# A decoder layer on one core: the last down-projection group made four tiles deep, and the next stage's first weights and rows prepared under its visits

## The reference, cut to what matters

```
gate, up = split(rmsnorm(h, g_ffn) @ w_gate_up)          # 2 x 5632 wide
h = h + (silu(gate) * up) @ w_down                       # "down"
h = h + sigmoid(rmsnorm(h, g_ple) @ w_ple_gate) * (p_i @ w_ple_proj)
y = rmsnorm(h, g_final)                                  # p_i is 256 wide
```

## Time and profile before

| | |
|---|---|
| median of 3 runs | 2339.3 us (2337.1 to 2341.42) |
| the profiled execution, its own time | 2344.21 us |
| span of the profiled execution | 2342.4 us |
| PE busy | 2270.8 us, 97% |
| DVE busy | 1639.2 us, 70% |
| ACT busy | 1080.8 us, 46% |
| POOL busy | 191.8 us, 8% |
| mean granted TensorE clock | 0.99 |

### The profile page before, as it was taken

How to read it: one execution, slowest core, us unless ns; L and a number is a source line. 1 busy time by engine, 2 the same in 40 slices (tenths; PEclk the granted TensorE clock), 3 DMA queues, 4 the chain that set the end, 5 groups by cost and what they waited for, 6 DMA issues and landing times.

```text
span 2342.4 us, 45807 instructions
## 1 busy us (share of the span) xinstructions
PE 2270.8 (97%) x18549; PEld 2219.8 (95%) x18549; DVE 1639.2 (70%) x2125; ACT 1080.8 (46%) x1639; POOL 191.8 (8%) x88
## 2 busy tenths in 40 slices
PE   7999999999999999999999999999899999989997
PEld 6988898888999999999999999999899999979997
DVE  5355555564257888888888888888777777885333
ACT  5334444443245455454445454554434444564434
POOL 0041112301221000000000000000000000121111
PEclk9999999999999999999999999999999999999999
DMA  7454565543334445454554545457966865532332
GB/s 251 141 167 155 163 195 179 175 122 128 93 90 150 119 134 171 139 171 139 161 149 136 160 132 161 136 171 224 299 178 191 235 179 148 148 90 82 88 107 80
DMA packets 488018, 359.44 MB, mean 153 GB/s; under 512 B 8417, under 2 KB 469298, under 8 KB 487001
## 3 DMA queue, kind: packets, MB, share of 16 engines
q1 hardware_dynamic: 474921, 347.31, 50.2%
q10 hardware_dynamic: 13000, 10.78, 1.4%
HBM read 301.23 MB, written 57.29 MB: 153 GB/s over the span
## 4 chain that ended last, share of the span: by engine, by line
PE 91%; DVE 4%; DMA 2%; ACT 2%; issue 1%; SPq 0%; ACTq 0%; DVEq 0%
PE acc L1161 39%; PE acc L718 30%; PE scores L1161 15%; PE scores L718 2%; PE mail_bank L718 1%; PE o_bank L718 1%; DMA x_low<-act_low_rows 1%; DVE w_low L2378 1%; DVE w_low L1932 1%; DMA region<-in_x_prompt 1%; PE mail_bank L882 0%; DVE raw L2382 0%; ACT w_high L1378 0%; DVE x_low L1940 0%; DMA raw<-in_w_ple_gate 0%
## 5 line engine op out<-in xcount | busy, mean ns | idle before, releaser
L1161 PE MATMUL acc<-x_high,w_high 128*128 128x260 f32 x1584 | 449.2, 284 | 9.0 <-DMA x_low<-act_low_rows 6.4
L718 PE MATMUL acc<-x_high,w_high 128*128 128x260 f32 (+2 forms) x2048 | 437.4, 291 | 11.0 <-DVE w_low L1932 6.3
L1161 PE MATMUL acc<-x_low,w_high 128*128 128x260 f32 x1584 | 448.0, 283 | 0.0
L1161 PE MATMUL acc<-x_high,w_low 128*128 128x260 f32 x1584 | 447.7, 283 | 0.0
L718 PE MATMUL acc<-x_high,w_low 128*128 128x260 f32 (+2 forms) x2048 | 421.8, 284 | 0.0
L718 PE MATMUL acc<-x_low,w_high 128*128 128x260 f32 (+2 forms) x2048 | 421.5, 284 | 0.0
L2378 DVE TENSOR_TENSOR w_low<-raw,w_high 128x1024 fp32r<-128x1024 f32 (+4 forms) x252 | 285.6, 1134 | 121.3 <-ACT w_high L1704 120.3
L718 PEld LDWEIGHTS acc<-x_high,w_high 128*128 128x128 f32 x2048 | 320.4, 190 | 33.8 <-issue 24.2
L2378 DVE TENSOR_TENSOR w_low<-key_pages,w_high 128x1024 fp32r<-128x1024 f32 (+4 forms) x252 | 283.5, 1132 | 89.0 <-ACT w_high L1704 88.0
L718 PEld LDWEIGHTS acc<-x_low,w_high 128*128 128x128 f32 x2048 | 321.0, 190 | 0.1
L718 PEld LDWEIGHTS acc<-x_high,w_low 128*128 128x128 f32 x2048 | 321.0, 190 | 0.0
(11 more groups left out here) (313 smaller groups left out, 4015.9 us busy)
## 6 DMA issues: line engine op xcount, KB each, us to landing
raw<-in_w_gate_up SPq DMA_DIRECT2D x44, 1024.0 KB, 6.8
key_pages<-in_w_gate_up SPq DMA_DIRECT2D x44, 1024.0 KB, 7.6
raw<-in_w_in SPq DMA_DIRECT2D x32, 1024.0 KB, 7.1
act_high_rows<-late_rounded SPq DMA_DIRECT2D x22, 910.0 KB, 5.3
act_low_rows<-late_rounded SPq DMA_DIRECT2D x22, 910.0 KB, 7.0
key_pages<-in_cache_k SPq DMA_DIRECT2D x32, 512.0 KB, 5.9
late<-in_cache_v SPq DMA_DIRECT2D x32, 512.0 KB, 6.0
raw<-in_w_out SPq DMA_DIRECT2D x16, 1024.0 KB, 5.8
```

The costliest lines, as they stand in the source:

```text
L718: return pe.matmul(o, l, r, start=start, stop=stop)
L1161: return pe.matmul(bank, w, x, start=start and first, stop=last, skip_group_check=True)
```

## The change

1. **Groups.** `GROUPS` goes from (4, 4, 4, 4, 3, 3) to (4, 4, 4, 3, 3, 4). The depths of the seven blocks go from 4, 8, 8, 8, 7, 6, 3 to 4, 8, 8, 7, 6, 7, 4.
2. **Quarters.** The first two gate slabs are loaded in four quarters each, laid out by `place_of`. The two "early" quarters of each (tiles 8 to 11 and 0 to 3) are loaded behind the weights of the last block's first visit, into places that a four-deep visit leaves free; the rest after the next-to-last visit's parts. ACT and DVE make an early quarter's high and low part, and one row's, behind windows 25 and 26 (of 0 to 27), and the rest after the last window, between rows.
3. **Order of tiles.** `first_two` takes the tiles in `X_ORDER`, one of each slab in turn. The first two tiles of slab 0 wait only for the additions of the visit before the last, and the statistics come behind eight tiles of both.
4. **p.** It is turned behind twelve tiles (rows) of both slabs, after the root; its small transposes go to a free place of the scores' bank.
5. **Third and fourth slab.** They are written out ahead of the loop, with the first turning of y inside the third slab.
6. The sums of squares of this stage move to `rstd` and `region`.

```diff
-GROUPS = (4, 4, 4, 4, 3, 3)
-FIRST = (0, 4, 8, 12, 16, 19)
+GROUPS = (4, 4, 4, 3, 3, 4)
+FIRST = (0, 4, 8, 12, 15, 18)
+X_ORDER = (8, 9, 10, 11, 0, 1, 2, 3, 12, 13, 14, 15, 4, 5, 6, 7)
+def place_of(k):
+    return k // 8 * 8 + (k + 4) % 8
...
-        sum_sq_ple = x_plain[1][:, KD - 1, :]
+        sum_sq_ple = rstd[:, :]
...
+            def load_ple(early):                                  # SP
+                for s in (0, 1):
+                    for a in (1, 0):
+                        k = a * HK + (0 if early else HK // 2)
+                        sp.dma_start(quarter_of(raw[s], early, a)..., w_pg_v[:, k:k + HK // 2, s * P:(s + 1) * P]).then_inc(ple_landed[s], 16)
...
                 load_down(n)
+                if n == ALL - 4:
+                    load_ple(True)
...
             sp.wait_ge(S["part_low"], 7 * (ALL - 1))
-            for s in (0, 1):
-                load(Slab(PLE_N + s), w_pg_v[:, :, s * P:(s + 1) * P])
+            load_ple(False)
...
+            def first_two():                                      # PE
+                pe.wait_ge(S["added"], 6 * (ND - 1))
+                pe.wait_ge(S["first_low"], 1)
+                tile(0, 0)
+                tile(0, 1)
+                pe.wait_ge(S["added"], 6 * ND)
+                pe.wait_ge(S["first_low"], 2)
+                tile(1, 0)
+                tile(1, 1)
+                for n in range(2, HK):
+                    if n == 4:
+                        pe.wait_ge(S["first_low"], 4)
+                    tile(0, n)
+                    tile(1, n)
+                stats(2)
+                pe.wait_ge(S["w_low_done"], PLE_N + 1)
+                tile(0, HK)
+                pe.wait_ge(S["w_low_done"], PLE_N + 2)
+                tile(1, HK)
+                for n in range(HK + 1, KD):
+                    if n == HK + 4:
+                        pe.wait_ge(S["root_ready"], 2)
+                        turn_p()
+                    tile(0, n)
+                    tile(1, n)
...
-            pe.wait_ge(S["added"], 6 * ND)
-            turn_p()
...
             project(0, 1)
+            slab, t = Slab(PLE_N + 2), PLE_T + 2
+            begin(slab, t)
+            part_of(slab, acc[0], t, range(0, 4))
             turn_y(0, 0)
-            with pe.Fori(1, KD // 2 - 1) as j:
+            part_of(slab, acc[0], t, range(4, 12))
+            turn_y(1, 1)
...
                 elif v > ND - 8:                                  # ACT
-                    extra = lambda: squares_of(v - 1)
+                    def extra():
+                        squares_of(v - 1)
+                        if v in (ND - 3, ND - 2):
+                            first_weights(v - ND + 3, 1)
+                            x_high(X_ORDER[v - ND + 3], V_PLE)
...
-            act.wait_ge(S["prod_done"], 7 * ALL - 1)
-            high(Slab(PLE_N))
+            for n in (2, 3):
+                x_high(X_ORDER[n], V_PLE)
+            first_weights(0, 0)
+            first_weights(1, 0)
+            for n in range(4, HK):
+                x_high(X_ORDER[n], V_PLE)
             squares_of(ND - 1)
+            rest_weights(0, 1, "rest_high")
+            rest_weights(0, 0, "w_high_done")
+            rest_weights(1, 1, "rest_high")
+            rest_weights(1, 0, "w_high_done")
...
-            norm_high(2, V_PLE, Slab(PLE_N + 1))
+            for k in X_ORDER[HK:HK + 4]:
+                x_high(k, V_PLE)
+            root(2)
+            for k in X_ORDER[HK + 4:]:
+                x_high(k, V_PLE)
...
                     window(n, n % 2, landings_of(n, n % 2), q, "down", 2 * ((v - 1) % 8))   # DVE
+                if v in (ND - 3, ND - 2):
+                    first_low(v - ND + 3, 1, v - ND + 4)
+                    ple_row(v - ND + 3)
...
-            low(Slab(PLE_N))
+            ple_row(2)
             add_down(ND - 1, 5, last, 0)
             add_down(ND - 1, 6, last, 0)
+            ple_row(3)
+            first_low(0, 0, 3)
+            first_low(1, 0, 4)
+            for n in range(4, HK):
+                ple_row(n)
+            rest_low(0, 1, 1, "rest_high", "rest_low")
+            rest_low(0, 0, PLE_N + 1, "w_high_done", "w_low_done")
+            rest_low(1, 1, 2, "rest_high", "rest_low")
+            rest_low(1, 0, PLE_N + 2, "w_high_done", "w_low_done")
+            for n in range(HK, HK + 4):
+                ple_row(n)
+            invert_root(2)
+            for n in range(HK + 4, KD):
+                ple_row(n)
+            V.wait()
...
             dve.wait_ge(S["p_turned"], 1)
-            norm_low(2, V_PLE, Slab(PLE_N + 1))
```

More of the change, by code:

```diff
@@ L403, in cells, with quarter_of @@
             return x[:, a * HT:b * HT]
+        def quarter_of(x, early, a):
+            at = a * HS + (HK // 2 * P if early else 0)
+            return x[:, at:at + HK // 2 * P]
         views = [(xh[:, 0:HK, 0:HT], xl[:, 0:HK, 0:HT]), (xt_h[:, 1], xt_l[:, 1]), (xt_h[:, 2], xt_l[:, 2]),
@@ L455, in layer @@
         act_stored = sem("act_stored")
+        ple_landed = [sem(f"ple_slab_landed{i}") for i in range(2)]
         h_back = [sem(f"h_back{i}") for i in range(3)]
@@ L645, in load_operand @@
                         .then_inc(op_landed[i], 16)
+            def load_ple(early):
+                for s in (0, 1):
+                    for a in (1, 0):
+                        k = a * HK + (0 if early else HK // 2)
+                        sp.dma_start(quarter_of(raw[s], early, a).rearrange("p (k n) -> p k n", n=P),
+                                     w_pg_v[:, k:k + HK // 2, s * P:(s + 1) * P]).then_inc(ple_landed[s], 16)
             def load_wp(j):
@@ L1236, in turn_p, with tile @@
                         pe.transpose(bank[:, b * P:(b + 1) * P], p_nat[:, b, k * P:(k + 1) * P], ident)
-                    ins = pe.transpose(sc[:, 0, k * NB:(k + 1) * NB], ps_nat[:, k * P:(k + 1) * P], ident[0:NB, 0:NB])
+                    ins = pe.transpose(sc[:, 0, SC_P + k * NB:SC_P + (k + 1) * NB], ps_nat[:, k * P:(k + 1) * P], ident[0:NB, 0:NB])
                 ins.then_inc(S["p_turned"], 1)
[L1240 to L1253, removed]
+            def first_two():
+                def tile(s, n):
+                    k = X_ORDER[n]
+                    if s == 0:
+                        pe.wait_ge(S["x_low"], 2 * KD + n + 1)
+                    col = slice(place_of(k) * P, (place_of(k) + 1) * P)
+                    ins = product(acc[s], wh[s][:, col], wl[s][:, col], xh[:, k, :], xl[:, k, :], n == 0, n == KD - 1)
+                    if n == KD - 1:
+                        ins.then_inc(S["acc_ready"], 1)
+                pe.wait_ge(S["added"], 6 * (ND - 1))
[22 more added lines that the diff above has]
+                    tile(1, n)
@@ L1261, in _ @@
                 visit(0, v % 2, NS + v)
-            for b in range(1, BLOCKS):
+            for b in range(1, BLOCKS - 1):
                 with pe.Fori(0, 2) as j:
@@ L1265, in _ @@
                         visit(b, i, 2 * j + (NS + 4 * b + i))
-            pe.wait_ge(S["added"], 6 * ND)
-            turn_p()
+            for v in range(ND - 4, ND):
+                visit(BLOCKS - 1, v % 2, NS + v)
             def project(j, s):
@@ L1305, in _ @@
             project(0, 1)
+            slab, t = Slab(PLE_N + 2), PLE_T + 2
+            begin(slab, t)
+            part_of(slab, acc[0], t, range(0, 4))
             turn_y(0, 0)
-            with pe.Fori(1, KD // 2 - 1) as j:
+            part_of(slab, acc[0], t, range(4, 12))
+            turn_y(1, 1)
+            part_of(slab, acc[0], t, range(12, KD))
+            project(1, 0)
+            slab, t = Slab(PLE_N + 3), PLE_T + 3
+            begin(slab, t)
+            part_of(slab, acc[1], t, range(0, KD // 2))
+            turn_y(2, 0)
+            part_of(slab, acc[1], t, range(KD // 2, KD))
+            project(1, 1)
+            with pe.Fori(2, KD // 2 - 1) as j:
                 ple(j)
@@ L1647, in _ @@
             act.wait_ge(S["v_stored"], 16 * NH)
[L1649 to L1656, removed]
             def t_scale(k, *which):
@@ L2296, in out_step @@
                     low(Slab(OUT_N + c + 2))
-            def norm_low(phase, gain, slab):
-                for k in range(KD):
-                    if k == LEAD:
-                        low(slab)
-                    if k == LEAD + 3:
-                        invert_root(phase)
-                    norm_split(phase, gain, KD * phase, k)
-                V.wait()
             def t_sums(k):
```

31 lines of the change are left out of this document (25 added, 6 removed).

## The result

| | before | after |
|---|---|---|
| median of 20 runs each | 2341.25 us (2337.1 to 2346.08) | 2344.73 us (2341.65 to 2350.33) |
| span of the profiled execution | 2342.4 us | 2345.0 us |
| mean granted TensorE clock | 0.990 | 0.987 |

The ratio of after to before is 1.0017, with a 95% interval from 1.001 to 1.0024. The change costs some 3.5 us. That is within the 0.2% that I called no change, but my 2338.6 us is 6.1 us too low, and 2344.73 lies above the range's 2342.5. Of the 6.1 us, 1.95 are the starting point: the kernel before has a median of 2341.25 us in 20 runs, against 2339.3 in the three shown. The other 4.2 are mine: I forecast 0.7 us gained, and 3.5 were lost.

What follows compares the result with a forecast made beforehand. TensorE, busy 97% of the span, was taken as the bound, so only its idle places could give time: 0.5 (last block) - 2.5 (block 5) + 2.7 (transition) = 0.7 us gained, median 2338.6 us, range 2332.5 to 2342.5.

Steps and rivals of the forecast that it cites:

- Block 5: Block 5's operand fetches: fifth pair late by 1.8 us, sixth and seventh add 0.7; cost 2.5 us, from 0 to 4.
- X+24.5: Landing of block 5's fifth operand pair, X being the issue of the group's first; its product starts at X+22.7.
- my 1.8: Block 5: us by which the fifth operand pair comes late for its product.
- the slower rival: Block 5: operand wait drops the clock, 2.0 us more from about 3 us on; 2344.5 us; chance 0.10.
- The last block: Four-deep last block, two visits with extra quarter and row: loses 6.3 instead of 6.8 us; gain 0.5, bounds -1.5 to 3.7.
- the hold of the row: Last block, behind windows 25 and 26: VectorE's row takes 0.66 us and about 1.0 held by GpSimd's second sum.
- The transition: From the last block's end past the third slab's start: 5.2 - 0.5 - 2.0 = 2.7 us gained; bounds 0.7 and 4.7.
- E+35.8: Start of the third gate slab, E being the last block's end; instead of 41.0 us, so 5.2 gained.
- Given back: Behind the third slab's start: turning y 0.5 us, and four us at half speed after nearly 7 us idle, 2.0.
- the third slab's load comes last: Transition: the third slab can start only after wp's low part, whose wait SP puts ahead of its load.

Runs made afterwards that it cites:

- e1: The kernel before with only the groups changed to 4, 4, 4, 3, 3, 4 and the sums-of-squares scratch moved; median 2342.32 us, ratio 1.0002 to before.
- e3: The changed kernel with the two quarters and two input rows done behind the last window, not under visits 25 and 26; 2347.43 us, ratio 1.0018 to before.
- e5: The changed kernel with the third and fourth slab's loads issued ahead of SyncE's wait for w_p's first low halves; 2337.26 us, ratio 0.9979 to before.
- e7: The kernel before with only the third and fourth slab's loads issued ahead of SyncE's wait; 2340.99 us, ratio 1.0001 to before.
- after again: The changed kernel run and profiled once more, unaltered; 2345.58 us, ratio 1.0011 to before.
- e10: The changed kernel with the slab loads ahead of SyncE's wait and the last group's seven operand pairs ahead of the weights; 2338.47 us, ratio 0.9987 to before.
- e6: The changed kernel with groups 4, 4, 3, 4, 3, 4, early slab loads, and quarters and rows behind the last window; 2333.90 us, ratio 0.9965 to before.
- e9: The changed kernel with the last group's seven operand pairs all issued ahead of the second visit's weights; 2345.38 us, ratio 1.0012 to before.
- e4: The changed kernel with groups 4, 4, 3, 4, 3, 4, so the three-deep groups stand apart; 2343.38 us, ratio 1.0005 to before.
- e8: The changed kernel with groups 4, 4, 3, 4, 3, 4 and the third and fourth slab's loads ahead of SyncE's wait; 2334.38 us, ratio 0.9965 to before.
- e2: The changed kernel with the old groups 4, 4, 4, 4, 3, 3, the rest of the change kept; 2347.63 us, ratio 1.0022 to before.
- e12: The changed kernel with the old groups, quarters and rows behind the last window, and early slab loads; 2339.67 us, ratio 0.9987 to before.

## Why the prediction was wrong

*Block 5, the step that failed.* I put the cost at 2.5 us, from 0 to 4; it came to 4.1. The wait was where I put it, in the fifth product; the low half landed at 1979.58 + 7.95 = 1987.53, which is X+24.9 with X = 1962.61, against my X+24.5. The timeline of SyncE shows the weights between the fourth and the fifth pair:

```profile
1962.61 0.37 SPq L659 DMA_DIRECT2D x_high<-act_high_rows  x1
...
1969.46 0.53 SPq L659 DMA_DIRECT2D x_low<-act_low_rows  x1
1970.03 7.95 SPq L652 DMA_DIRECT2D key_pages<-in_w_down  x4
...
1979.58 0.93 SPq L659 DMA_DIRECT2D half_sums_low<-act_low_rows  x1
```

What was wrong is the price of being late, and 1.6 us are missing in it. Some 0.9 of them come without any fall of the clock, as e1 shows with 3.4: the fifth pair was 0.4 later than my 1.8, and the sixth and seventh added up to some 1.2 instead of 0.7. My own figures would have given that: 3.1 us on the wire less 2.5 on PE is 0.6 for each of the two pairs. The other 0.5 to 0.7 are the clock. I let it fall only "from about 3 us on", in the slower rival, a number that no run shows, and it fell behind 2.2 us. The rival's full 2.0 on top would have been too much, since e1's later waits shrink under the slower clock.

*The last block.* Forecast 0.5 gained, measured 0.1 lost, inside my bounds. The mechanism held: the period of the visits with extras is 12.97 us (2063.78, 2076.75), forecast 12.8. The rows of one such visit:

```profile
2063.78 0.36 PE L1185 MATMUL acc<-half_sums_high,w_high 128*128 128x260 f32 x1 [0.88 <-DVE w_low L2443]
...
2067.45 3.03 POOL L2737 TENSOR_TENSOR rstd<-rstd,region 128x520 f32<-128x520 f32 x2 [8.39 <-ACT region L1443]
...
2068.36 0.94 DVE L2618 TENSOR_TENSOR w_low<-raw,w_high 128x512 fp32r<-128x512 f32 x1 [0.88 <-ACT w_high L1873]
2069.23 1.80 DVE L2612 SCALAR_TENSOR_TENSOR x_low<-late,gains,x_high 128x520 fp32r<-128x520 f32 x1
...
2076.75 0.36 PE L1185 MATMUL acc<-half_sums_high,w_high 128*128 128x260 f32 x1 [0.86 <-DVE w_low L2443]
```

The quarter takes 0.94 us and the row 1.80 us beside GpSimd's two sums, which end at 2070.48; where no sum runs beside them they take 0.68 and 0.75. Two rows of e3 show that:

```profile
2095.89 0.75 DVE L2612 SCALAR_TENSOR_TENSOR x_low<-late,gains,x_high 128x520 fp32r<-128x520 f32 x1
...
2097.24 0.68 DVE L2618 TENSOR_TENSOR w_low<-raw,w_high 128x512 fp32r<-128x512 f32 x1
```

I had the hold of the row, not that of the quarter. The Trainium skill (SBUF — State Buffer, "SBUF: two separate sides") describes a lock that makes a VectorE instruction with two SBUF inputs wait for a GpSimd instruction that reads SBUF; the quarter and the row both have two. The trace agrees: both are longer, and the row ends at 2071.03, 0.55 us after GpSimd's second sum.

*The transition.* E+35.5, forecast E+35.8; 6.15 us idle, forecast nearly 7. Given back: 3.3 behind the slab, forecast 2.5. The clock took 1.5 (e5 against after: 190.73 - 189.27), the turning of y its 0.5, and 0.9 to 1.0 was a wait that I had not: the first turning of y at line 1332, now inside the third slab, comes before ScalarE has its rows. The kernel before has that wait at line 1288, ahead of its third slab; I moved the turning in my sum and forgot its wait. Some 0.3 of the 3.3 stay without a cause. So 2.2 gained, not 2.7. That the third slab's load comes last was right, and e5 with e7 shows that it costs something only because of the change.

*The end.* 1.5 us at line 1393 for which nothing in the change is the cause that I could find. All 14 profiled executions have the same 1.98 to 1.99 us wait there; behind it the clock fell in four (after, after again, e3, e10). It is left open why the changed kernel did so in both of its profiles.

*The sum.* Block 5 1.6, last block 0.6, transition 0.5, end 1.5: the 4.2 us between -0.7 and +3.5.

## What to carry to other kernels

When a late start is removed, ask which transfer it covered: here one load behind one wait in a queue was worth nothing in the old kernel and 6 us in the new one (e7, e5). Work put "under" a stage that runs in a loop of hand-overs is not hidden because its engine has idle time; e3 and e6 show that it costs the same 3 us on either side. And when one stage is made shorter and the next one's data larger, count bytes over the time between the two visits first: the other order of the queue only moved the wait (e9), while other depths halved the cost (4.1 to 2.2 us, e4 and e8).

## What the runs showed of the hardware

A wait of 2 us on TensorE can already bring the clock to 0.50, the 1.2 GHz level, but does so only sometimes. Over the 14 profiles:

- behind the waits of 1.98 to 1.99 us at the end it fell in 4 of 14;
- behind 2.07 to 2.34 us in block 5 it fell in 3 of 5 (after, after again and e5; not e1 and e3, though e3's wait of 2.30 was longer than after's 2.20);
- behind 2.9 and 3.0 us it fell in 2 of 2 (e9, e10);
- behind one wait of 1.92 us (e2) it fell, behind one of 1.70 (e12) not;
- with 5.6 us and more at the third slab it fell in 6 of 6 (after, after again, e2, e3, e4, e9).

The single wait is not the whole story. In e7 and e12 the clock fell inside the last down block, where no wait was over 1.0 us. Here are e7's longest wait there and the window behind it (its longer waits, 4.2 us at the turning of p, come later):

```profile
2071.40 0.41 PE L1165 MATMUL acc<-half_sums_high,w_high 128*128 128x260 f32 x1 [0.88 <-DVE w_low L2382]
...
2071.62:2075.02 3.40, 3.40 (x17) 3.40 (x17) 2.72 (x7) 1.96 (x5) 0.00 (x0) 0.50 0.00 0
```

The kernel before has the same waits and no fall there, and seven profiles with waits of 1.5 to 1.6 us in that block have none either. What sets the two cases apart is not shown.

Once fallen behind the short waits the clock stayed at 0.50 for about 3 us, some 1.5 us lost; at the end of e3 it stayed for 6.8 us, and 2.4 were lost. The Trainium skill (TensorE: Matmul & The Clock Gate, Part 1) says that the window in which the gate watches TensorE is free-running and does not reset when a kernel starts, so that the moment of a change depends on where in it the work falls. A fall that comes and goes with the same wait agrees with that, but no run here shows the window itself.
